# mLSTM gates by lanes of a direction, head and block of 128 tokens in place of rows

## The chip, the cores and the metric

One Trainium2 chip, one core. The number that counts is the device time of one execution of the kernel in microseconds (us). TensorE (PE) does matmuls and transposes, VectorE (DVE), ScalarE (ACT) and GpSimd (POOL) do elementwise work, SyncE (SP) and ACT issue the DMAs of this kernel. Each engine works through its own list of instructions in order and waits on semaphores for the others.

## The reference

Two layers of a backbone over 256 context tokens and 1024 latent tokens (1280 in all, ten tiles of 128), width 1024. Each layer normalizes, projects into the inputs of four head groups and a gate path, runs the groups, and projects back. The change touches the second group, the bidirectional mLSTM with four heads of 64:

```python
def _mlstm_step(state, xs):
    ...
    b = jnp.cumsum(lf, axis=-1)
    d = jnp.where(tril, b[..., :, None] - b[..., None, :] + li[..., None, :], -jnp.inf)
    m_inter = b + m[..., None]
    m_t = jnp.maximum(m_inter, jnp.max(d, axis=-1))
    w = jnp.exp(d - m_t[..., None])
    g_inter = jnp.exp(m_inter - m_t)
    ...
    h = num / jnp.maximum(jnp.abs(nq), jnp.exp(-m_t))[..., None]
    ...
    w_end = jnp.exp(g - m_new[..., None])
    decay = jnp.exp(b_end + m - m_new)
...
def mlstm_mixer(pl, pc, conv_w, conv_b, gate_b, outn_g, with_ctx):
    ...
        qk = jax.nn.silu(short_conv(jnp.concatenate([q, k], axis=-1), conv_w, conv_b))
    ...
        fwd = base + (pre[0], jax.nn.log_sigmoid(pre[1]))
        bwd = base + (pre[2], jax.nn.log_sigmoid(pre[3]))
```

Per token, direction and head there are an input gate `li` and a forget gate `lf`. What the recurrence needs of them is a running sum `b` of the log forget gates, a running maximum `m_t`, and four exponentials made from these.

## The kernel before

Each layer is a row of stages (modulation, norm, mLSTM, GLA, differential attention, window attention, gates, output) with a barrier of all engines behind each, and the engine programs in a stage are written out by hand. The mLSTM stage (`stage_mlstm`) has three blocks, each again ended by all engines: the projection block (the one changed), the recurrence over ten tiles in two directions, and `turn_out`.

The projection block runs `SplitProduct`, a product of the activations `hT` with weights in float32 split in a high and a low part. It has four groups of eight steps, written (g, k) here and in the code. In each step ACT makes the high part of the activations (`high`, tile `b_proj_xh`), DVE makes the high and low parts of the weights and the low part of the activations (`low`, tiles `b_proj_wh`, `b_proj_wl`, `b_proj_xl`), and PE multiplies (`multiply`). There are two buffers, so ACT and DVE may prepare step i when PE has finished step i-2. Groups 0 and 1 make the values `v` and the gates for five tiles of tokens each, with `WV` weight columns (15 matmuls a step). Groups 2 and 3 make the keys and the queries, transposed, for all 1280 tokens (18 matmuls a step, 12 with 512 columns and 6 with 256). The sums of a group are kept by ACT (`keep`) in the next group's step 1, behind that step's `high`; PE's first matmul of a group waits for the first of them, since the sums rotate through six PSUM banks.

Between the steps stand other pieces. In group 2 PE turns the gates into rows (`turn_gates`), 36 rows with 8 in use (direction and head) and 1280 tokens each, ACT adds the bias (`keep_gates`) and starts log sigmoid, DVE sums over each tile (`gate_sums`, behind `low` of (2, 6)) and runs the maxima and the joins of the tile ends (`gate_rows`, behind `low` of (3, 0)). Then DVE convolves the keys (`convolve`, behind (3, 2) and (3, 4)) and finishes their silu (`silu_k`, behind (3, 5) and (3, 7)). Behind the last step stand: the convolutions and silu of the queries on DVE; on PE 40 turns of the gate rows back to tokens, a small product for `decay`, and 20 turns of the keys; on ACT two sigmoids, the exponentials of the gates (16 pieces) and ten copies of turned keys (`ktm`).

The order is thus fixed by hand through the place of each piece between the steps, for example:

```python
                    if (g, k) == (2, 6):
                        gate_sums()
                    if (g, k) == (3, 0):
                        gate_rows()
```

Of the kernel before, what the change touches and what calls it, by code (L numbers as in the profile page):

```python
# [42 lines left out]
ROWS = 36  # L43
BLOCKS = [(0, 512), (512, 512), (1024, 256)]
# [8 lines left out]
SLAB_W = [512] * 4 + [328, 512, 288, 256, 512, 256, 512, 256, 512, 512] + [512] * 2 + [512] * 2  # L53
# [431 lines left out]
def stage_mlstm(nc, env):  # L485
    ps, signal, yT, ring = (env[n] for n in ("ps", "signal", "yT", "ring"))
    outer = ExitStack()
    with outer:
        v1 = outer.enter_context(env["sbuf"]("b_v", [P, NT, HEADS, DH + 1], F32))
        qkT = outer.enter_context(env["sbuf"]("b_qkT", [P, 4, T], F32))  # L490

        after = lambda s_, n: ring[:, s_ % RING, KT * SLAB_W[s_]:KT * SLAB_W[s_] + n]
        cols = after(S_CQK, NT * 4 * ROWS).rearrange("p (t q r) -> p t q r", t=NT, q=4)
        row_d = after(S_CV, T)[0:ROWS, :]
        row_a, row_c, row_e, row_b = (yT[0:ROWS, i, :] for i in range(4))
# [1954 lines left out]
```

## Time and profile before

| | us |
|---|---|
| median of 3 runs | 2687.75 |
| fastest, slowest | 2673.01, 2691.18 |
| the profiled execution | 2683.7 |
| its span in the trace | 2681.9 |
| projection block, layer 0 | 64.5 to 221.2 |
| projection block, layer 1 | 1435.3 to 1588.0 |

Times in rows are from the start of the profiled execution's span. Over the whole span PE is busy for 80% and DVE for 70%, but these are averages over stages with different limits; the projection blocks have to be read by themselves. A granted clock of TensorE is given as a share of full speed, 2.4 GHz.

### The profile page before, as it was taken

Reading aid. Unit: us, or ns where it says so; the run is one execution under the profiler, and the core shown is the slowest. Engines: PE = TensorE matmul, PEld = TensorE weight load, DVE = VectorE, ACT = ScalarE, POOL = GpSimd, SP = SyncE. Lnnn points to the kernel's source line nnn. Section 1 sums busy time; section 2 is a strip of 40 time slices with the busy share of each in tenths; the row PEclk is TensorE's granted clock in tenths of the full one; section 3 lists DMA queues with packets and bytes.
Section 4 is the critical chain, followed back from the end, with each engine's and each line's share of the span. In section 5 each row is a group of like instructions: output and inputs, shape, how many; then the busy total and the mean of one; then the engine's idle time right before and its main releaser. Section 6 shows DMA issues by size and latency. Waiting matters only on the chain. (4 is left out here: it accounts for less than half of the span.)

```text
span 2681.9 us, 38569 instructions
## 1 busy us (share of the span) xinstructions
PE 2151.8 (80%) x14712; PEld 1804.3 (67%) x14712; DVE 1867.3 (70%) x3533; ACT 1129.8 (42%) x2196; POOL 411.4 (15%) x410
## 2 busy tenths in 40 slices
PE   4968798786888785899978778879767977858988
PEld 2857676666677664787857567767655866647877
DVE  2585667778878567755745766669698786667757
ACT  4433351333667534633224443432435666346321
POOL 0002204322000011022110004025031000110222
PEclk7978896898898797999988889969788989979999
DMA  8100010000000100001433000100000001000021
GB/s 322 74 16 1 17 48 2 2 1 1 1 1 1 48 32 1 29 36 39 153 138 120 16 16 2 48 16 2 1 0 1 1 1 48 16 17 27 37 104 54
DMA packets 18182, 99.80 MB, mean 37 GB/s; under 512 B 2128, under 2 KB 2256, under 8 KB 12752
## 3 DMA queue, kind: packets, MB, share of 16 engines
q1 hardware_dynamic: 12816, 87.89, 8.6%
q10 hardware_dynamic: 5184, 9.44, 0.9%
q8 instruction: 119, 1.95, 0.3%
q14 instruction: 63, 0.52, 0.1%
HBM read 87.88 MB, written 9.44 MB: 36 GB/s over the span
## 5 line engine op out<-in xcount | busy, mean ns | idle before, releaser
L1807 DVE TENSOR_REDUCE a_st<-ps 128x1 f32<-128x1280 f32 (+1 forms) x144 | 196.9, 1370 | 23.2 <-PE ps L1719 22.7
L1778 ACT ACTIVATE ring<-ps,a_st 128x1280 f32<-128x1280 f32 (+1 forms) x144 | 177.3, 1232 | 74.6 <-DVE a_st L1807 74.4
L454 PE MATMUL ps<-a_proj_wh,a_proj_xh 128*128 128x512 f32 (+1 forms) x320 | 119.2, 373 | 62.5 <-DVE a_proj_xl L435 61.6
L2090 PE MATMUL ps<-g_x_hi,g_w_hi 128*128 128x512 f32 (+1 forms) x400 | 148.4, 371 | 10.0 <-DVE g_x_lo L2151 9.5
L2091 PE MATMUL ps<-g_x_lo,g_w_hi 128*128 128x512 f32 (+1 forms) x400 | 147.7, 369 | 0.0
L2092 PE MATMUL ps<-g_x_hi,g_w_lo 128*128 128x512 f32 (+1 forms) x400 | 147.6, 369 | 0.0
L1719 PE MATMUL ps<-a_k,a_q 128*128 128x512 f32 (+1 forms) x400 | 123.8, 419 | 26.1 <-ACT ring L1778 21.6
L2151 DVE TENSOR_TENSOR g_x_lo<-hT,g_x_hi 128x512 fp32r<-128x512 f32 (+1 forms) x120 | 84.5, 709 | 85.3 <-ACT g_x_hi L2114 83.8
L2114 ACT ACTIVATE g_x_hi<-hT 128x512 fp32r<-128x512 f32 (+1 forms) x120 | 70.3, 589 | 158.3 <-PE ps L2092 151.2
L1734 PE MATMUL ps<-cst,ring 128*128 128x128 f32 x656 | 107.8, 299 | 27.0 <-ACT a_aT L1787 15.1
L418 ACT ACTIVATE b_proj_xh<-hT 128x640 fp32r<-128x640 f32 (+1 forms) x64 | 63.8, 1003 | 147.4 <-PE ps L454 145.0
L2225 PE MATMUL ps<-o_w_hi,o_y_hi 128*128 128x512 f32 x288 | 114.1, 396 | 13.5 <-DVE o_y_lo L2256 7.2
L2164 POOL TENSOR_TENSOR yT<-yT,g_gate 128x512 f32<-128x512 f32 (+1 forms) x50 | 61.3, 1232 | 382.5 <-DVE g_gate L2129 236.7
L454 PEld LDWEIGHTS ps<-a_proj_wh,a_proj_xh 128*128 128x128 f32 x320 | 68.7, 215 | 75.3 <-issue 48.9
L454 PE MATMUL ps<-a_proj_wl,a_proj_xh 128*128 128x512 f32 (+1 forms) x320 | 116.2, 363 | 0.0
L454 PE MATMUL ps<-a_proj_wh,a_proj_xl 128*128 128x512 f32 (+1 forms) x320 | 115.8, 362 | 0.0
L2226 PE MATMUL ps<-o_w_lo,o_y_hi 128*128 128x512 f32 x288 | 113.5, 394 | 0.0
L2227 PE MATMUL ps<-o_w_hi,o_y_lo 128*128 128x512 f32 x288 | 113.3, 393 | 0.0
L1734 PEld LDWEIGHTS ps<-cst,ring 128*128 128x128 f32 x656 | 81.4, 153 | 46.5 <-ACT a_aT L1787 22.9
L454 PE MATMUL ps<-b_proj_xh,b_proj_wh 128*128 128x512 f32 (+1 forms) x192 | 76.9, 401 | 44.4 <-DVE b_proj_xl L435 38.0
L418 ACT ACTIVATE a_proj_xh<-hT 128x640 fp32r<-128x640 f32 x64 | 46.6, 741 | 147.9 <-PE ps L454 145.6
L2282 ACT ACTIVATE o_y_hi<-yT 128x640 fp32r<-128x640 f32 (+1 forms) x64 | 43.5, 686 | 152.5 <-PE ps L2227 144.6
(363 smaller groups left out, 6397.9 us busy)
## 6 DMA issues: line engine op xcount, KB each, us to landing
ring<-in_w SPq DMA_DIRECT2D x22, 2048.0 KB, 7.5
yT<-in_w SPq DMA_DIRECT2D x4, 2048.0 KB, 9.8
latents<-hT ACTq DMA_DIRECT2D x32, 256.0 KB, 2.0
ring<-in_w SPq DMA_DIRECT2D x6, 1024.0 KB, 5.0
hT<-in_tok SPq DMA_DIRECT2D x10, 512.0 KB, 15.5
hT<-in_tok SPq DMA_DIRECT2D x20, 256.0 KB, 5.9
hT<-latents SPq DMA_DIRECT2D x16, 256.0 KB, 6.5
cst<-in_cst SPq DMA_DIRECT2D x1, 2688.0 KB, 14.6
```

What stands on the lines that cost most here:

```text
L418: act.activation(self.x_hi[:, i % self.BUFS, 0:m], self.env["hT"][:, k, t0:t0 + m], ACT.Copy).then_inc(self.hi.sem, 1)
L454: last = pe.matmul(out, left, right, start=k == 0 and j == 0, stop=k == KT - 1 and j == 2)
L1719: last = pe.matmul(ps[:, 3 * c + b, 0:w], q4[:, 2 * h + c, t * P:(t + 1) * P], k4[:, 2 * h + c, k0:k0 + w], start=True, stop=True)
L1734: last = pe.transpose(ps[:, 6 + n % 2, (k - a) * P:(k - a + 1) * P], p(u, 0, T)[:, k * P:(k + 1) * P], C(env, "ident"))
L1778: act.activation(p(u, c, n), ps[:, 3 * c:3 * c + 3, :].rearrange("p b n -> p (b n)")[:, 0:n], ACT.Exp, bias=st[:, 0:1], accum_out=st[:, 1: ...
L1807: dve.tensor_reduce(stat[:, u % SLOTS, c, 0:1], ps[:, 3 * c:3 * c + 3, :].rearrange("p b n -> p (b n)")[:, 0:n], AX.X, ALU.max, negate=Tru ...
L2090: pe.matmul(out, w_hi[:, k, cols], x_hi[:, at, 0:b[1]], start=k == 0, stop=False)
L2091: pe.matmul(out, w_hi[:, k, cols], x_lo[:, at, 0:b[1]], start=False, stop=False)
L2092: last = pe.matmul(out, w_lo[:, k, cols], x_hi[:, at, 0:b[1]], start=False, stop=k == KT - 1)
L2225: pe.matmul(ps[:, n % 8, :], y_hi[:, at, tile], w_hi[:, at, :], start=k == 0, stop=False)
L2226: pe.matmul(ps[:, n % 8, :], y_hi[:, at, tile], w_lo[:, at, :], start=False, stop=False)
L2227: last = pe.matmul(ps[:, n % 8, :], y_lo[:, at, tile], w_hi[:, at, :], start=False, stop=k == KT - 1)
```

## The change

The gates no longer stand as 8 rows of 1280 tokens but as lanes: one partition for each direction, head and tile of 128 tokens, 104 partitions wide with 80 in use (40 of a direction from partition 0, 40 from partition 64), each 128 long. The projection makes 16 gate columns without gaps, so `WV` is 272 in place of 328. ACT puts the gates of a tile into four columns a direction of `gt`, and two transposes turn all of them. The sums and the maxima within a tile are then four scans of 40 lanes by 128. The ends of the tiles are joined on 36 rows by 10: `ends_by_row` moves each lane's end to its row and tile through a product with a 0/1 matrix (`lane_row`), `tile_peaks` runs the maxima over ten tiles, and `back_to_lanes` brings the results back through `row_lane`. The exponentials are taken on lanes (`exps`, in ACT's place (3, 0)), where ACT also issues 20 DMAs, each of 4 partitions by 128 elements, that bring one quantity (`g_cm`) back to rows for the recurrence. Four transposes turn the lanes to tokens (`turn_lanes`, PE's place (3, 1)), and two ACT instructions keep them (`keep_lanes`). The keys are turned two tiles at a time into a bank of their own and kept by five ACT instructions between the sigmoids of the queries. POOL clears two more pieces of `yT`.

```diff
-SLAB_W = [512] * 4 + [328, 512, 288, 256, 512, 256, 512, 256, 512, 512] + [512] * 2 + [512] * 2
+SLAB_W = [512] * 4 + [272, 512, 288, 256, 512, 256, 512, 256, 512, 512] + [512] * 2 + [512] * 2
...
-        after = lambda s_, n: ring[:, s_ % RING, KT * SLAB_W[s_]:KT * SLAB_W[s_] + n]
...
+        cols = ring[:, S_CV % RING, KT * SLAB_W[S_CV]:KT * SLAB_W[S_CV] + 4 * LANES].rearrange("p (q r) -> p q r", q=4)
+        lane_at = lambda i: yT[0:LANES, 0, i * P:(i + 1) * P]
+        g_a, g_b, g_t, g_c, g_e, g_m, g_cm, g_inter, g_floor, g_end = (lane_at(i) for i in range(10))
+        row_b = yT[0:ROWS, 3, :]
         ends = outer.enter_context(env["sbuf"]("b_ends", [ROWS, 4, NT], F32))
         decay = outer.enter_context(env["sbuf"]("b_decay", [P, 4, NT], F32))
-        conv_in = yT[:, 4:8, :]
+        conv_in = [yT[:, c, :] for c in (1, 2, 6, 7)]
         ktm = yT[:, 4:6, :].rearrange("p a t -> p (a t)").rearrange("p (t c) -> p t c", t=NT)
         hB = yT[:, 0:2, :].rearrange("p a t -> p (a t)").rearrange("p (t h d) -> p t h d", t=NT, h=HEADS)
-        gt = yT[:, 7, 0:NT * 2 * ROWS].rearrange("p (t r) -> p t r", t=NT)
+        gt = yT[:, 7, 0:2 * P].rearrange("p (q r) -> p q r", q=2)
+        gt_of = lambda t: gt.rearrange("p q (w r) -> p q w r", w=2)[:, :, :, 4 * t:4 * t + 4]
...
-        WV = GW + 2 * ROWS
+        WV = GW + 4 * HEADS
...
-                def turn_gates(n):
...
+                def turn_gates():
+                    pe.wait_ge(proj.read.sem, NT)
+                    pe.wait_ge(mod_kept.sem, 2)
+                    for q in range(2):
+                        last = pe.transpose(ps[0:LANES, 6, q * P:(q + 1) * P], gt[:, q, 0:LANES], C(env, "ident"))
                     last.then_inc(gates_turned.sem, 1)
+                def ends_by_row():
+                    pe.wait_ge(ends_cut.sem, 4)
+                    pe.matmul(ps[0:ROWS, 7, 0:2 * NT], C(env, "lane_row", LANES), cut_at[0:LANES, :, :].rearrange("p a t -> p (a t)"),
+                              start=True, stop=True).then_inc(ends_mm.sem, 1)
+                def back_to_lanes():
+                    pe.wait_ge(peaks_ready.sem, 1)
+                    pe.matmul(ps[0:LANES, 7, P:P + 2 * NT], C(env, "row_lane", ROWS),
+                              ends[:, 0:3:2, :], start=True, stop=True, skip_group_check=True).then_inc(back_mm.sem, 1)
+                def turn_lanes():
+                    pe.wait_ge(lane_exps.sem, 4)
+                    pe.wait_ge(lanes_ready.sem, 1)
+                    for q, x in enumerate((g_a, g_inter, g_floor, g_end)):
+                        last = pe.transpose(ps[:, 6, q * LANES:(q + 1) * LANES], x, C(env, "ident")[0:LANES, 0:LANES])
+                    last.then_inc(lanes_turned.sem, 1)
...
+                def keep_gates():
+                    act.wait_ge(v_ones.sem, 4)
+                    act.wait_ge(gates_turned.sem, 1)
+                    act.activation(g_a, ps[0:LANES, 6, 0:P], ACT.Identity, bias=W(env, "gate_li", LANES)).then_inc(act_l.sem, 1)
+                    act_l.n += 1
+                    act_l.link(act, act.activation(g_b, ps[0:LANES, 6, P:2 * P], ACT.Identity, bias=W(env, "gate_lf", LANES)))
+                    act_l.link(act, act.activation(g_t, g_b, ACT.Abs))
+                    act_l.link(act, act.activation(g_t, g_t, ACT.Exp, scale=-1.0))
+                    act_l.mark(act.activation(g_t, g_t, ACT.Ln, bias=1.0))
+                def exps():
+                    act.wait_ge(lanes_ready.sem, 1)
+                    act.activation(g_inter, g_cm, ACT.Exp, bias=lane_ends[0:LANES, 1:2]).then_inc(lane_exps.sem, 1)
+                    act.activation(g_floor, g_m, ACT.Exp, scale=-1.0).then_inc(lane_exps.sem, 1)
+                    act.activation(g_end, g_a, ACT.Exp, bias=lane_ends[0:LANES, 0:1]).then_inc(lane_exps.sem, 1)
+                    act.activation(ends[:, 3, :], ends[:, 3, :], ACT.Exp).then_inc(lane_exps.sem, 1)
+                    for way in range(2):
+                        for t in range(NT):
+                            act.dma_start(row_b[32 * way:32 * way + HEADS, t * P:(t + 1) * P],
+                                          g_cm[64 * way + HEADS * t:64 * way + HEADS * (t + 1), :]).then_inc(row_moved.sem, 16)
+                def keep_lanes():
+                    act.wait_ge(lanes_turned.sem, 1)
+                    act.activation(cols[:, :, :], ps[:, 6, 0:4 * LANES].rearrange("p (q r) -> p q r", q=4), ACT.Copy).then_inc(lanes_kept.sem, 1)
+                    act.wait_ge(lanes_turned.sem, 2)
+                    act.activation(decay[:, :, :], ps[:, 7, 0:4 * NT].rearrange("p (a b) -> p a b", a=4), ACT.Copy).then_inc(lanes_kept.sem, 1)
+                def keep_k(n):
+                    act.wait_ge(turned.sem, n + 1)
+                    act.activation(ktm[:, 2 * n:2 * n + 2, :].rearrange("p t c -> p (t c)"), ps[:, 6 + n % 2, :], ACT.Copy).then_inc(turned_kept.sem, 1)
...
-                    if g == 2 and k in (2, 3, 4):
...
+                    if (g, k) == (2, 2):
+                        keep_gates()
+                    if (g, k) == (3, 0):
+                        exps()
+                    if (g, k) == (3, 2):
+                        keep_lanes()
                     if g == 3 and k in (4, 6):
                         sigmoid(2 if k == 4 else 3)
                 for n in range(proj.first[-2], proj.first[-1]):
                     keep(n)
-                for c in range(2):
...
+                keep_k(0)
+                keep_k(1)
+                sigmoid(0)
+                keep_k(2)
+                sigmoid(1)
+                keep_k(3)
+                keep_k(4)
+                act.wait_ge(turned_kept.sem, NT // 2)
+                act.wait_ge(row_moved.sem, 2 * NT * 16)
...
-                    dve.wait_ge(act_l.sem, 3)
                     dve.wait_ge(env["const_loaded"].sem, 16)
-                    dv.link(dve, dve.scalar_tensor_tensor(out=row_b, in0=row_b, scalar=0.0, in1=row_c,
...
+                    dve.wait_ge(act_l.sem, 5)
+                    dv.link(dve, dve.scalar_tensor_tensor(out=g_b, in0=g_b, scalar=0.0, in1=g_t, op0=ALU.min, op1=ALU.subtract))
+                    ones, tiles = C(env, "ones"), C(env, "lane_tile")
+                    for i, (r, at) in enumerate(WAYS):
+                        x = (lambda y: y[r, :]) if i == 0 else (lambda y: y[r, ::-1])
+                        dv.mark(dve.tensor_tensor_scan(x(g_c), ones[r, :], x(g_b), 0.0, ALU.mult, ALU.add))
+                        dv.link(dve, dve.tensor_tensor_scan(x(g_e), x(g_b), x(g_a), NEG, ALU.add, ALU.max))
+                        for j, y in enumerate((g_c, g_e)):
+                            dve.tensor_scalar(cut_at[r, j, :], tiles[r, :], y[r, at:at + 1], None, ALU.mult).then_inc(ends_cut.sem, 1)
+                def tile_peaks():
+                    dve.wait_ge(ends_mm.sem, 1)
+                    dv.mark(dve.memset(ends[:, 1:4, :], 0.0))
+                    dv.link(dve, dve.tensor_copy(ends[:, 0, :], ps[0:ROWS, 7, 0:NT]))
+                    c, e, m = ends[:, 0, :], ps[0:ROWS, 7, NT:2 * NT], ends[:, 1, :]
+                    b = slice(32, ROWS)
+                    dv.mark(dve.tensor_tensor_scan(m[0:HEADS, :], c[0:HEADS, :], e[0:HEADS, :], 0.0, ALU.add, ALU.max))
+                    dv.link(dve, dve.tensor_tensor_scan(m[b, 0:NC][:, ::-1], c[b, 0:NC][:, ::-1], e[b, 0:NC][:, ::-1], 0.0, ALU.add, ALU.max))
+                    dv.link(dve, dve.tensor_tensor_scan(m[b, NC:NT][:, ::-1], c[b, NC:NT][:, ::-1], e[b, NC:NT][:, ::-1],
+                                                        m[b, 0:1], ALU.add, ALU.max))
...
                     dv.link(dve, dve.tensor_tensor(ends[:, 0, :], ends[:, 0, :], ends[:, 1, :], ALU.subtract))
                     dv.link(dve, dve.tensor_tensor(ends[:, 3, :], ends[:, 0, :], ends[:, 2, :], ALU.add))
-                    wide = lambda i: ends[:, i, :].unsqueeze(2).broadcast_to([ROWS, NT, P])
...
+                    dve.sem_inc(peaks_ready.sem, 1)
+                def lanes():
+                    dve.wait_ge(back_mm.sem, 1)
+                    r = slice(0, LANES)
+                    dv.mark(dve.tensor_tensor(g_a, g_a, g_c, ALU.subtract))
+                    dv.link(dve, dve.tensor_tensor(back[r, :, :], ps[r, 7, P:P + 2 * NT].rearrange("p (a t) -> p a t", a=2),
+                                                   C(env, "lane_tile", LANES).unsqueeze(1).broadcast_to([LANES, 2, NT]), ALU.mult))
+                    dv.link(dve, dve.tensor_reduce(lane_ends[r, :], back[r, :, :], AX.X, ALU.add))
+                    dv.link(dve, dve.scalar_tensor_tensor(out=g_m, in0=g_c, scalar=lane_ends[r, 1:2], in1=g_e, op0=ALU.add, op1=ALU.max))
+                    dv.link(dve, dve.tensor_tensor(g_cm, g_c, g_m, ALU.subtract))
+                    dve.sem_inc(lanes_ready.sem, 1)
 
...
+                dv.link(dve, dve.memset(cut_at[:, :, :], 0.0))
                 for n in range(2):
                     dve.memset(ps[:, 6 + n, :], 0.0).then_inc(mod_cleared.sem, 1)
                 for i, (g, k) in enumerate(proj.steps):
                     proj.low(dve, i)
-                    if (g, k) == (2, 6):
+                    if (g, k) == (2, 3):
                         gate_sums()
-                    if (g, k) == (3, 0):
-                        gate_rows()
+                    if (g, k) == (2, 5):
+                        tile_peaks()
+                    if (g, k) == (2, 7):
+                        lanes()
...
-                return cols[:, j, q, 32 * way:32 * way + HEADS]
+                return cols[:, q, 64 * way + HEADS * j:64 * way + HEADS * (j + 1)]
...
+                lane, row = 64 * way + HEADS * t + h, 32 * way + h
+                put("lane_row")[lane, row] = 1.0
+                put("row_lane")[row, lane] = 1.0
+                put("lane_tile")[lane, t] = 1.0
...
-        slabs += [np.concatenate([take(*B_V), li, lf], 1), take(*B_QK),
+        slabs += [np.concatenate([take(*B_V)] + [gates[:, i] for i in (0, 2, 1, 3)], 1), take(*B_QK),
```

The first place is DVE behind `low` of (2, 6) and (3, 0), before (`yT`, `ring` hold the gate rows, `b_ends` the tile ends):

```order
L674 SCALAR_TENSOR_TENSOR yT<-yT 36x1280
...
L681 SCALAR_TENSOR_TENSOR yT<-cst,yT 4x128
L683 SCALAR_TENSOR_TENSOR yT<-cst,yT 4x128
...
L687 SCALAR_TENSOR_TENSOR ring<-yT 4x1280
L689 SCALAR_TENSOR_TENSOR ring<-yT 4x256
L691 SCALAR_TENSOR_TENSOR ring<-yT,ring 4x1024
...
L706 TENSOR_TENSOR yT<-yT 36x1280
L707 TENSOR_TENSOR yT<-yT,ring 36x1280
L708 TENSOR_TENSOR yT<-yT,b_ends 36x1280
L709 TENSOR_TENSOR yT<-yT,b_ends 36x1280
```

The same engine in the changed kernel, behind `low` of (2, 3) and of (2, 7) (`b_cut` and `b_back` are the operands of the 0/1 products):

```order
L706 SCALAR_TENSOR_TENSOR yT<-yT 104x128
L710 SCALAR_TENSOR_TENSOR yT<-cst,yT 40x128
L711 SCALAR_TENSOR_TENSOR yT<-yT 40x128
L713 TENSOR_SCALAR b_cut<-cst,yT 40x10 x2
...
L736 TENSOR_TENSOR yT<-yT 104x128
L737 TENSOR_TENSOR b_back<-ps,cst 104x20
L739 TENSOR_REDUCE b_lane_ends<-b_back 104x2
L740 SCALAR_TENSOR_TENSOR yT<-yT,b_lane_ends 104x128
L741 TENSOR_TENSOR yT<-yT 104x128
```

The long rows became short ones, in three pieces in place of two (behind (2, 5) stand eleven more of at most 36 by 30), all of them behind steps of group 2.

The second place is ACT between the `high` of (3, 0) and of (3, 1) in the changed kernel; before, nothing stood there:

```order
L633 ACT_TABLE_LOAD
L633 ACTIVATE yT<-yT,b_lane_ends 104x128
L634 ACTIVATE yT<-yT 104x128
L635 ACTIVATE yT<-yT,b_lane_ends 104x128
L636 ACTIVATE b_ends<-b_ends 36x10
L639 DMA yT<-yT 4x128 x20
L420 ACTIVATE b_proj_xh<-hT 128x1280
```

So the exponentials and 20 DMA issues now stand ahead of that `high`. The third place is ACT behind the last kept sums, before:

```order
L613 ACTIVATE yT<-b_qkT 128x1280 x2
L638 ACT_TABLE_LOAD
L638 ACTIVATE b_ends<-b_ends 36x10
L644 ACTIVATE ring<-ps 128x3x36 x12
L644 ACTIVATE ring<-ps 128x36 x4
L647 ACTIVATE b_decay<-ps 128x40
L651 ACTIVATE yT<-ps 128x256 x10
```

and in the changed kernel:

```order
L650 ACTIVATE yT<-ps 128x512 x2
L655 ACTIVATE yT<-b_qkT 128x1280
L650 ACTIVATE yT<-ps 128x512
L655 ACTIVATE yT<-b_qkT 128x1280
L650 ACTIVATE yT<-ps 128x512 x2
```

Nothing of the gates is left there, and of the ten copies of keys five wider ones, three of them ahead of the second sigmoid.

## Rows read from the trace of the kernel before

**Rows 1.** Windows, both layers: length, busy PE, PEld, DVE, ACT, POOL (instructions), PE clock, DMA.

```profile
64.50:106.80 42.30, 38.66 (x245) 36.44 (x249) 25.95 (x50) 13.78 (x27) 0.17 (x1) 0.92 0.31 117
...
158.60:203.40 44.80, 35.26 (x145) 29.04 (x145) 36.82 (x51) 17.96 (x22) 0.00 (x0) 0.81 0.07 24
203.40:221.20 17.80, 8.62 (x68) 8.17 (x68) 10.19 (x11) 9.76 (x31) 0.05 (x1) 0.62 0.00 0
...
1435.30:1476.60 41.30, 37.77 (x245) 35.57 (x249) 25.95 (x50) 13.69 (x27) 0.07 (x1) 0.96 0.31 120
...
1528.00:1569.70 41.70, 32.01 (x144) 26.36 (x144) 37.14 (x51) 18.05 (x22) 0.00 (x0) 0.92 0.08 26
```

**Rows 2.** DVE's timeline in group 0, and in the GLA stage's like group.

```profile
76.72 0.33 DVE L381 CAST b_proj_wh<-ring 128x328 fp32r<-128x328 f32 x1 [0.63 <-PE ps L454]
...
87.94 0.33 DVE L381 CAST b_proj_wh<-ring 128x328 fp32r<-128x328 f32 x1 [0.64 <-PE ps L454]
...
328.18 0.83 DVE L435 TENSOR_TENSOR c_proj_xl<-hT,c_proj_xh 128x640 fp32r<-128x640 f32 x1
...
340.24 0.83 DVE L435 TENSOR_TENSOR c_proj_xl<-hT,c_proj_xh 128x640 fp32r<-128x640 f32 x1
```

**Rows 3.** DVE's timeline, gate pieces of layer 0, start and length in us.

```profile
138.19 1.48 DVE L674 SCALAR_TENSOR_TENSOR yT<-yT 36x1280 f32<-36x1280 f32 x1
...
141.20 0.41 DVE L681 TENSOR_TENSOR_SCAN yT<-cst,yT 4x128 f32<-4x128 f32 x1
...
154.22 2.80 DVE L687 TENSOR_TENSOR_SCAN ring<-yT 4x1280 f32<-4x1280 f32 x1
...
160.15 0.16 DVE L695 COPY b_ends<-yT 4x10 f32<-4x10 f32 x1
...
166.04 1.48 DVE L709 TENSOR_TENSOR yT<-yT,b_ends 36x1280 f32<-36x1280 f32 x1
...
171.81 0.94 DVE L661 TENSOR_SCALAR b_qkT<-yT,par 128x1280 f32<-128x1280 f32 x1
```

**Rows 4.** PE's timeline: turns, (2, 7), (3, 0), (3, 6) and (3, 7).

```profile
119.11 1.04 PE L548 MATMUL ps<-cst,yT 128*36 128x128 f32 x8
...
152.39 0.76 PE L454 MATMUL ps<-b_proj_xh,b_proj_wh 128*128 128x512 f32 x1 [10.23 <-DVE b_proj_xl L435]
...
160.54 0.47 PE L454 MATMUL ps<-b_proj_xh,b_proj_wh 128*128 128x512 f32 x1 [1.94 <-ACT yT L598]
...
195.65 0.40 PE L454 MATMUL ps<-b_proj_xh,b_proj_wh 128*128 128x512 f32 x1
...
199.15 0.39 PE L454 MATMUL ps<-b_proj_xh,b_proj_wh 128*128 128x512 f32 x1
```

**Rows 5.** Window of step (2, 7), columns as in rows 1.

```profile
152.40:158.50 6.10, 6.10 (x18) 4.89 (x18) 6.00 (x6) 0.00 (x0) 0.00 (x0) 0.55 0.00 0
```

**Rows 6.** ACT's timeline: a `high`, and pieces at the end of the block.

```profile
158.64 1.27 ACT L418 ACTIVATE b_proj_xh<-hT 128x1280 fp32r<-128x1280 f32 x1 [15.17 <-PE ps L454]
...
212.42 1.28 ACT L638 ACT_TABLE_LOAD   x1
...
216.98 3.73 ACT L651 ACTIVATE yT<-ps 128x256 f32<-128x256 f32 x10 [0.84 <-PE ps L583]
```

**Rows 7.** DVE's timeline from the queries' convolution to the next block.

```profile
201.64 0.95 DVE L661 TENSOR_SCALAR b_qkT<-yT,par 128x1280 f32<-128x1280 f32 x1 [1.60 <-ACT yT L598]
...
211.19 2.89 DVE L734 TENSOR_TENSOR b_qkT<-b_qkT,yT 128x1280 f32<-128x1280 f32 x2
221.18 1.05 DVE L876 CAST b_row_parts<-yT 64x1280 fp32r<-64x1280 f32 x1 [7.09 <-PEq L516]
```

**Rows 8.** DMA issues by line: duration ns min/median/max, first and last start.

```profile
L2276 ACTq DMA_DIRECT2D latents<-hT x32: 338/338/374, 1309.6 to 2678.5; - x32
...
DMA to landing us min/median/max: 2.0/2.0/3.9
...
L2203 SPq DMA_DIRECT2D hT<-in_tok x20: 327/432/678, 1271.3 to 1281.1; - x20
```

More of the change, by code:

```diff
@@ L43 @@
 ROWS = 36
+LANES = 104
 BLOCKS = [(0, 512), (512, 512), (1024, 256)]
@@ new lines, in turn_lanes @@
+                def turn_lanes():
[4 more added lines that the diff above has]
+                    last.then_inc(lanes_turned.sem, 1)
+                    sel = C(env, "sel_pair", ROWS).rearrange("p (a b) -> p a b", a=4)
+                    for i in range(4):
+                        last = pe.matmul(ps[:, 7, i * NT:(i + 1) * NT], sel[:, i, :], ends[:, 3, :], start=True, stop=True)
+                    last.then_inc(lanes_turned.sem, 1)
@@ L558, in _ @@
                         modulate(pe, env, mod_w[:, k - 5, :, :], k + 1).then_inc(mod_mm.sem, 1)
-                    if g == 2 and k in (1, 2, 3):
-                        turn_gates(k - 1)
-                pe.wait_ge(proj.read.sem, proj.first[-1])
-                pe.wait_ge(rows_ready.sem, 1)
-                for t in range(NT):
-                    for q, r in enumerate((row_a, row_c, row_d, row_e)):
-                        at = (t % 3) * 4 * ROWS + q * ROWS
-                        last = pe.transpose(ps[:, 4 + t // 3, at:at + ROWS], r[:, t * P:(t + 1) * P],
-                                            C(env, "ident")[0:ROWS, 0:ROWS])
-                last.then_inc(turned.sem, 1)
-                pe.wait_ge(dec_ready.sem, 1)
-                sel = C(env, "sel_pair", ROWS).rearrange("p (a b) -> p a b", a=4)
-                for i in range(4):
-                    last = pe.matmul(ps[:, 0, i * NT:(i + 1) * NT], sel[:, i, :], ends[:, 3, :], start=True, stop=True)
-                last.then_inc(turned.sem, 1)
-                pe.wait_ge(silu_ready.sem, 4)
-                for t in range(NT):
-                    if t == 0:
-                        pe.wait_ge(turned_kept.sem, 17)
-                    if t >= 4:
-                        pe.wait_ge(turned_kept.sem, 17 + t - 3)
-                    for c in range(2):
-                        last = pe.transpose(ps[:, t % 4, c * P:(c + 1) * P], qkT[:, 2 + c, t * P:(t + 1) * P], C(env, "ident"))
+                    if (g, k) == (2, 1):
+                        turn_gates()
+                    if (g, k) == (2, 4):
+                        ends_by_row()
+                    if (g, k) == (2, 6):
+                        back_to_lanes()
+                    if (g, k) == (3, 1):
+                        turn_lanes()
+                pe.wait_ge(lanes_kept.sem, 2)
+                pe.wait_ge(silu_ready.sem, 2)
+                for n in range(NT // 2):
+                    if n >= 2:
+                        pe.wait_ge(turned_kept.sem, n - 1)
+                    for i in range(4):
+                        t, c = 2 * n + i // 2, i % 2
+                        last = pe.transpose(ps[:, 6 + n % 2, i * P:(i + 1) * P], qkT[:, 2 + c, t * P:(t + 1) * P], C(env, "ident"))
                     last.then_inc(turned.sem, 1)
@@ L2333, in constants @@
     put("ones")[:] = 1.0
+    for way in range(2):
+        for t in range(NT):
+            for h in range(HEADS):
+                lane, row = 64 * way + HEADS * t + h, 32 * way + h
+                put("lane_row")[lane, row] = 1.0
+                put("row_lane")[row, lane] = 1.0
+                put("lane_tile")[lane, t] = 1.0
     put("diag")[:] = (np.arange(P)[:, None] // 32) == (np.arange(GW)[None, :] // DH)
```

124 lines of the change are left out of this document (31 added, 93 removed).

## The prediction

> **What bounds the kernel now.** The change touches one block of one stage in each layer, and every block is ended by all engines together, so what that block loses or gains goes into the total one to one. I read it from the windows first [rows 1]: in the stretch of group 3 PE is busy 35.26 of 44.80 us and DVE 36.82, at a granted clock of 0.81, so neither is full and they take turns; in the last 17.80 us PE has 8.62 and DVE 10.19, a chain. In groups 0 and 1 PE is busy 38.66 of 42.30. The timelines say who sets the pace. In group 0 DVE's weight cast comes every 2.24 us (11.22 us over five steps) and waits for PE each time [rows 2]: PE is the bound. In group 2 PE stands 10.23 us before step (2, 7) for DVE's `low` [rows 4], because `gate_sums` runs on DVE from 138.19 [rows 3]; the low clock follows, and that step takes 6.10 us at clock 0.55 [rows 5], where a step at full clock takes 3.50 (195.65 to 199.15 [rows 4]). `gate_rows` then holds DVE from 154.22 to 167.5 [rows 3]. At the end DVE finishes the queries at 214.08 (211.19 + 2.89), but the next block starts at 221.18 [rows 7]: the last 7.1 us are ACT's exponentials and key copies, begun by a table load at 212.42 and ended by copies from 216.98 [rows 6].
>
> **Groups 0 and 1: narrower product.** `WV` goes from 328 to 272. The nearest row is the GLA stage, 288 columns: six steps from 328.18 to 340.24, 2.01 a step [rows 2]. Forty columns cost 0.23, so 272 gives 2.01 - 0.09 = 1.92, and a step gains 0.33. DVE's and ACT's work for a step (about 1.6) stays under that. Over 15 steps: **4.9 us a layer**. Bounds: 3.5 (0.23 a step, the price of 288 columns) to 5.7 (2.24 us over 328 columns, 0.0068 a column).
>
> **Group 2: the gate pieces, in layer 0's time, groups 0 and 1 left as they were.** Prices: a DVE step is 2.15 (two steps between 167.5 and 171.81 [rows 3]), `high` 1.27 [rows 6], a scan of 128 0.41 plus 0.03, a tiny DVE instruction 0.16 [rows 3], an ACT instruction of 128 columns 0.26 (from 1.27 for 1280 and 0.37 for 256 columns [rows 6]), a table load 1.28. The path:
> - (2, 1) ends on PE at 119.11, where the turns start. Eight turns took 0.8 of PE; two take 0.3. ACT then does five instructions and one table load, 119.75 to 122.5, and `high` of (2, 3) ends at 123.8; `low` at 125.25; PE runs (2, 3) 125.3 to 128.8.
> - `gate_sums` (0.3 + 4 scans + 4 tiny) 2.7 us to 127.95; `low` of (2, 4) to 130.1; PE 130.1 to 133.6, then the first 0/1 product to 133.85. `low` of (2, 5) is done at 132.2, so DVE idles 1.8 for that product.
> - `tile_peaks`, eleven tiny instructions, 1.75: to 135.75. `low` of (2, 6) to 137.9; PE (2, 5) to 137.4, (2, 6) to 141.4, the second product to 141.6. DVE waits again, 1.8.
> - `lanes`, five instructions, 1.25: to 143.05; PE (2, 7) from 141.6 to 145.1, ahead of DVE.
>
> So the long idle and its low clock are gone from (2, 7): 145.1 against 158.4. What is late next is ACT. `exps` waits for `lanes` (143.05), loads a table, does four instructions: 145.5. Then it issues 20 DMAs before `high` of (3, 1). An issue on ACT took 0.338 of its own [rows 8]; SP's run of 20 took 10.2 from first start to end, 0.51 each. These rows are all DMAs of 128 partitions; one of 4 partitions is in no row. I take 0.39 (0.338 and a gap of 0.05), since 0.33 is the floor whatever the bytes: 7.8 us, to 153.3. `high` starts then, and PE starts (3, 0) 1.90 behind it (158.64 to 160.54 [rows 4, 6]): 155.2 in place of 160.5, **gain 5.3**. Bounds for an issue: 0.05 (nothing but a gap), giving 148.4, and 0.51, giving 157.6.
>
> The Trainium skill, DMA: Bandwidth & Descriptors, section Anatomy of one DMA, gives for GpSimd's path about 50 ns of sequencer dispatch, with descriptor generation "small, variable". By that the 20 issues would cost 1.0 us and the gain of group 2 would be 12.1; the trace's issues from ACT and SP do not agree, at 0.33 and more.
>
> **Group 3.** From the start of (3, 0), T0. PE stood 10 us, so as at (2, 7) [rows 5] (3, 0) takes 6.0. DVE's `low` of (3, 2) waits for it and for `high`: done at T0 + 8.75. Convolution 4.75 (9.55 for two [rows 7]) to 13.5, `low` to 15.6, `low` of (3, 4) to 17.75, convolution to 22.5, `low` 24.65, silu 26.1, `low` 28.25; PE is then the bound, (3, 6) to 31.75 and (3, 7) behind it; the queries' convolution starts 2.5 later (199.15 to 201.64 [rows 4, 7]), at T0 + 34.25. Before it was T0 + 41.1: **gain 6.8** in layer 0. `turn_lanes` (about 1.0 on PE) and `keep_lanes` (0.8 on ACT) stand behind (3, 1) and (3, 2), where PE waits 1.6 for the convolution anyway: they cost nothing; without that cover 1.8.
>
> **The end.** The keys' turns and three of five copies lie under the 9.5 us of convolution; no exponentials remain. DVE's last product ends 12.45 behind the convolution's start as now (214.08 - 201.64 [rows 7]); barrier 0.4. 12.85 in place of 19.54: **gain 6.7**. The recurrence's first exponential needs a table load in the next block, where ACT waits for PE's warm-up. That warm-up follows a longer rest of PE: cost 0.5, bounds 0 and 2. The Trainium skill, ScalarE: Activation LUTs, section What ACT_TABLE_LOAD costs, adds a drain of about 1.38 us to each load; here the load took 1.28 and nothing more stood behind it [rows 6], so I leave it out. With it the load in `exps` would cost 1.4 more a layer, the sum 2.8 less.
>
> **The sum.** Layer 0: 4.9 + 5.3 + 6.8 + 6.7 - 0.5 = 23.2, so its block goes from 156.7 to 133.5. Layer 1's block was 152.7: it lost less to the clock, 1.4 in groups 0 and 1 (0.96 against 0.92 [rows 1]) which the changed kernel will save again, and 3.1 in group 3 (a stretch of 41.70 against 44.80, at 0.92 against 0.81 [rows 1]). Its new length is 133.5 - 1.4 = 132.1, gain 20.6. Together **43.8**: the profiled execution from 2683.7 to 2639.9. That execution lies 4 us below the median, so against the median 2687.75 the forecast is **2644**.
>
> **Rivals.**
> - **Issues are cheap.** Four partitions need fewer descriptors and fewer rings than any row. At 0.05 the issues are over at 146.5, T0 is 148.4, 6.8 earlier, and PE's rest is 3 us, so perhaps (3, 0) runs at full clock (2.5 more). Gain 43.8 + 13.6 to 18.6, time **2625 to 2630**. For it: nothing measured at that size. Against: no issue in [rows 8] took under 0.327.
> - **The short pieces are slow to hand over.** Three crossings DVE-PE-DVE and some 25 tiny instructions stand in line in group 2; 0.2 more for each is 5 us a layer, time **2654**. Against: tiny ones follow each other at 0.1 to 0.2.
> - **The clock stays low in group 3.** If it stays at 1.2 GHz in place of 2.4 after the rest in front of (3, 0), eight steps of 6.1 make it PE-bound: 48.8 + 2.5 against 34.25, reduced by what overlaps to 14 a layer; time **2672**. For it: 0.81 in layer 0. Against: 0.92 in layer 1 with the same rests [rows 1].
> - **Slower: the issues queue.** If each issue must wait until the one before has landed, 2.0 us [rows 8], 20 of them take 40 in place of 7.8 on ACT, T0 moves by 32 a layer, time **2708**. It decides from 1.5 us an issue on (0.39 + 22/20). Against: ACT's stores land in 2.0 but hold it 0.34.
> - **Nothing gained but the width**: if a wait I have not seen, such as the row transfers at the block's end, covers the rest: 2678.
>
> **How the numbers follow.** Forecast (2636 to 2650) 0.50; cheap issues 0.25; slow handovers 0.13; low clock 0.06; queued issues 0.03; only the width 0.03. The range from 2622 to 2660 leaves out the last three. A change of 1% (27 us, about what a measurement of this kernel can tell from none) is at 2661: faster 0.88, same 0.08, slower 0.04.
>
> **What the profile after will show.** Step period 1.92 in group 0; PE's start of (2, 7) without a wait of 10 us; 20 issues on ACT between `high` of (3, 0) and of (3, 1), with PE idle behind them for 10 us (rival one: 3); 12.9 from the queries' convolution to the next block. Wrong it would be made by the price of an issue above all: each 0.1 is 4 us of the total. Next is the clock in group 3, 2.5 us for each slow step on the path.

## The result and the profile after

The changed kernel takes **2638.94 us** (median of 4, 2634.85 to 2641.88), the kernel before 2684.22 on the same chip (median of 4): ratio 0.9833, 95% interval 0.9806 to 0.986, 45.3 us less. The forecast was 2644. One execution that is read below, the profiled one of the eight longer issues, ran at a granted clock of 0.54 throughout and took 3546 us; it counts in no median. The profiled execution of the changed kernel took 2636.4. The head of its page, then the new issues on ACT's queue, by line:

```profile
span 2634.6 us, 38349 instructions
PE 2109.6 (80%) x14612; PEld 1765.6 (67%) x14612; DVE 1827.8 (69%) x3505; ACT 1117.2 (42%) x2156; POOL 413.4 (16%) x414
L639 ACTq DMA_DIRECT2D yT<-yT x40: 584/585/1180, 139.9 to 1500.9; - x40
```

The shares are averages over all stages and say little here. The last line says most: each new issue held ACT for 0.585 us (584/585/1180 are minimum, median and maximum in ns). Layer 0's block by windows, in place of [rows 1]: groups 0 and 1, group 2, the rest in front of (3, 0), group 3, the end (busy time and count of PE, PEld, DVE, ACT, POOL, then the granted clock, the DMA share and GB/s):

```profile
66.20:104.40 38.20, 36.29 (x261) 32.36 (x262) 25.95 (x50) 14.26 (x27) 0.36 (x1) 0.91 0.34 135
104.40:141.20 36.80, 32.93 (x163) 27.10 (x162) 23.13 (x50) 17.06 (x30) 1.98 (x2) 0.95 0.00 1
141.20:154.69 13.49, 0.02 (x1) 0.03 (x1) 1.38 (x4) 1.90 (x3) 0.00 (x0) 0.63 0.01 3
154.69:188.40 33.71, 30.77 (x151) 25.80 (x152) 25.21 (x31) 15.32 (x19) 0.00 (x0) 0.95 0.09 32
188.40:201.30 12.90, 3.84 (x27) 2.92 (x25) 11.86 (x12) 6.48 (x10) 0.00 (x0) 0.79 0.00 0
```

One hole is left, the third row: 13.5 us in which no engine does much. The timeline of ACT names its owner:

```profile
137.29 1.27 ACT L420 ACTIVATE b_proj_xh<-hT 128x1280 fp32r<-128x1280 f32 x1 [2.96 <-PE ps L456]
138.59 1.28 ACT L633 ACT_TABLE_LOAD   x1
139.88 0.40 ACT L633 ACTIVATE yT<-yT,b_lane_ends 104x128 f32<-104x128 f32 x1
...
140.69 0.19 ACT L636 ACTIVATE b_ends<-b_ends 36x10 f32<-36x10 f32 x1
141.10 11.64 ACTq L639 DMA_DIRECT2D yT<-yT  x19
152.79 1.27 ACT L420 ACTIVATE b_proj_xh<-hT 128x1280 fp32r<-128x1280 f32 x1 [11.91 <-issue]
```

On PE's timeline, the turns of the gates in layer 0 and the first matmul of (3, 0) in layer 1:

```profile
114.14 0.38 PE L554 MATMUL ps<-cst,yT 128*104 128x128 f32 x2
...
1503.46 0.77 PE L456 MATMUL ps<-b_proj_xh,b_proj_wh 128*128 128x512 f32 x1 [12.91 <-ACT yT L618]
```

PE rested 12.91 us in front of (3, 0) in layer 1. DVE's timeline gives the step pitch of group 0, one short piece of each kind in group 2, the queries' convolution and the next block's first row in each layer (answering to [rows 2, 3, 7]):

```profile
77.83 0.30 DVE L383 CAST b_proj_wh<-ring 128x272 fp32r<-128x272 f32 x1 [0.41 <-PE ps L456]
...
85.62 0.30 DVE L383 CAST b_proj_wh<-ring 128x272 fp32r<-128x272 f32 x1 [0.39 <-PE ps L456]
...
120.48 0.42 DVE L710 TENSOR_TENSOR_SCAN yT<-cst,yT 40x128 f32<-40x128 f32 x1
...
129.41 0.08 DVE L717 MEMSET b_ends<- 36x30 f32 x1 [0.90 <-PE ps L559]
...
137.58 0.29 DVE L736 TENSOR_TENSOR yT<-yT 104x128 f32<-104x128 f32 x1 [1.72 <-PE ps L564]
...
188.41 0.95 DVE L693 TENSOR_SCALAR b_qkT<-yT,par 128x1280 f32<-128x1280 f32 x1 [1.59 <-ACT yT L618]
...
201.37 1.04 DVE L911 CAST b_row_parts<-yT 64x1280 fp32r<-64x1280 f32 x1 [0.53 <-PEq L521]
...
1549.91 1.04 DVE L911 CAST b_row_parts<-yT 64x1280 fp32r<-64x1280 f32 x1 [0.53 <-PEq L521]
```

The block took 201.37 - 64.5 = 136.9 us (before 156.7) and in layer 1, begun at 1415.3, 134.6 (before 152.7): 19.8 and 18.1 us less, 37.9 together, where I had forecast 43.8. The spans differ by 47.3. So the block gave less than forecast, and something outside it gave 9.4.

### The profile page after: what moved, and what is told of

Same layout as the page of the kernel before. It is cut to its first block and busy times, and to the rows that moved or that the text cites. A ratio compares the mean times of both kernels' runs of the same rounds, so it can differ in the third digit from the quotient of the medians.

```text
span 2634.6 us, 38349 instructions
## 1 busy us (share of the span) xinstructions
PE 2109.6 (80%) x14612; PEld 1765.6 (67%) x14612; DVE 1827.8 (69%) x3505; ACT 1117.2 (42%) x2156; POOL 413.4 (16%) x414
## 5 line engine op out<-in xcount | busy, mean ns | idle before, releaser
L1754 PE MATMUL ps<-a_k,a_q 128*128 128x512 f32 (+1 forms) x400 | 123.8, 419 | 25.8 <-ACT ring L1813 21.3
L1241 ACT ACTIVATE yT<-ps 128x1024 f32<-128x1024 f32 x40 | 41.0, 1024 | 153.5 <-PE ps L1259 153.5
```

Of the source, the lines that this page charges most:

```text
L1754: last = pe.matmul(ps[:, 3 * c + b, 0:w], q4[:, 2 * h + c, t * P:(t + 1) * P], k4[:, 2 * h + c, k0:k0 + w], start=True, stop=True)
```

## Experiments

Unless said otherwise each differs from the changed kernel by the edit shown, and "more" or "less" is against its median, 2638.94. The kernel before had medians of 2679.64 and 2679.13 beside the experiments, 5 us below the 2684.22 beside the changed kernel, so a difference of totals alone is good to about 5 us. What the two projection blocks took in the profiled execution of each kernel is a second measure. It agrees with the totals to 3 us, except for the kernel before:

| kernel | layer 0 | layer 1 | both, against the changed kernel | total, against it |
|---|---|---|---|---|
| before | 156.7 | 152.8 | +37.9 | +45.3 (more on it at the end of this section) |
| changed | 136.9 | 134.6 | | |
| issues on SP | 123.7 | 125.1 | -22.8 | -24.3 |
| 8 issues on SP | 125.0 | 123.8 | -22.8 | -23.6 |
| 20 more issues | 147.5 | 148.0 | +24.0 | +25.3 |
| width given back | 142.4 | 141.2 | +12.0 | +12.3 |
| rest kept warm | 136.6 | 134.5 | -0.5 | +2.1 |
| turns at the end | 140.7 | 138.7 | +7.9 | +7.7 |

**The issues on SP,** between its loads of the values' and the keys' weights, and taken out of `exps`.

```diff
+                sp.wait_ge(lanes_ready.sem, 1)
+                for way in range(2):
+                    for t in range(NT):
+                        sp.dma_start(row_b[32 * way:32 * way + HEADS, t * P:(t + 1) * P],
+                                      g_cm[64 * way + HEADS * t:64 * way + HEADS * (t + 1), :]).then_inc(row_moved.sem, 16)
...
-                            act.dma_start(row_b[32 * way:32 * way + HEADS, t * P:(t + 1) * P],
```

> The changed kernel with its 20 row transfers issued by SP in place of ACT, behind SP's wait for the lanes. Theory (the issues hold ACT, and ACT's high of (3, 1) holds PE): the rest of PE in front of (3, 0) falls from 13.5 us to about 2, since (2, 7) ended at 141.2 and a high and the first kept sum take 1.9; (3, 0) starts at about 143.2 in place of 154.7, and runs at full clock. Gain 11.5 to 14 us a layer, 23 to 28 together, time 2611 to 2616 where the changed kernel has 2639. Rival (the transfers or the exponentials, not the issues, hold the chain): the start of (3, 0) stays within 2 us of 154.7 and the time within 5 of 2639.

Measured 2614.65 (2612.82 to 2617.13), ratio 0.9756 (0.9742 to 0.9771) to the kernel before, 24.3 less than the changed one. SP's issues, PE's first matmul of (3, 0), and the next block:

```profile
L537 SPq DMA_DIRECT2D yT<-yT x40: 577/577/712, 137.2 to 1485.9; - x40
...
141.34 0.47 PE L456 MATMUL ps<-b_proj_xh,b_proj_wh 128*128 128x512 f32 x1 [1.94 <-ACT yT L624]
...
187.88 1.05 DVE L913 CAST b_row_parts<-yT 64x1280 fp32r<-64x1280 f32 x1 [0.54 <-PEq L521]
```

An issue costs SP the same 0.577, and nobody waits for it. PE's rest is 1.94 us in place of 13.5, and the next block of layer 0 comes 13.5 earlier. The 20 issues in ACT's path are what the changed kernel left lying: 12 us a layer (13.2 and 9.6 by the blocks). One part of the expectation failed: (3, 0) did not run at full clock, see the warm rest below.

**Fewer, longer issues:** 8 of 10 partitions into one, still on ACT.

```diff
-                        for t in range(NT):
-                            act.dma_start(row_b[32 * way:32 * way + HEADS, t * P:(t + 1) * P],
-                                          g_cm[64 * way + HEADS * t:64 * way + HEADS * (t + 1), :])
+                        for h in range(HEADS):
+                            act.dma_start(row_b[32 * way + h:32 * way + h + 1, :].rearrange("p (t i) -> p t i", t=NT),
+                                          g_cm[64 * way + h:64 * way + HEADS * NT:HEADS, :])
```

> The changed kernel with 8 transfers on ACT in place of 20, the same data: one for each direction and head, from 10 partitions (one for each tile) to one partition. Theory (a fixed price for each issue, 0.585 in the changed kernel): 8 of them take about 4.9 us in place of 12.3, (3, 0) starts about 7.3 earlier, gain 15 together, 2624. Rival (the price goes with rows or descriptors, 80 in both): an issue takes about 1.4, nothing is gained, 2639.

```profile
L639 ACTq DMA_DIRECT2D yT<-yT x16: 725/731/1324, 176.4 to 2000.6; - x16
```

Measured 2626.03 (2624.28 to 2628.41), ratio 0.9797 (0.9781 to 0.9813), 12.9 less, where the fixed price of 0.585 promised 15. Of its profile only the issues count. An issue of this shape costs 0.73, neither 0.585 nor the 1.4 of the rival; 8 x 0.73 is 5.8 in place of 12: half of what SP gives. Both steps together, these 8 on SP:

> The changed kernel with 8 transfers, one for each direction and head, issued by SP. If the issues on ACT were all that held (3, 0), it is as fast as 20 issues from SP, 2611 to 2616; if the transfers' end or the load of the next slab behind them on SP matters, it is some us faster than that.

```profile
L537 SPq DMA_DIRECT2D yT<-yT x16: 718/719/850, 138.7 to 1485.0; - x16
```

Measured 2615.3 (2613.02 to 2616.14), the same as 20 on SP, and the two blocks together are the same too. Between 8 and 20 on SP the number of issues has no price.

**What an issue costs by kind:** 20 more issues on ACT behind the 20, four of each kind, to unused places: 4, 16, 128 and 1 partitions from SBUF, then 4 partitions from DRAM. The first and the last of the five loops:

```diff
+                    for n in range(4):
+                        act.dma_start(spare(slice(0, 4), n), C(env, "ident", 4)).then_inc(kinds.sem, 16)
...
+                    for n in range(4):
+                        act.dma_start(spare(slice(0, 4), 16 + n), env["dram"]["cst"][0:4, 0:P]).then_inc(kinds.sem, 16)
```

> The changed kernel with 20 more issues on ACT behind the first 20, four each of five kinds, of constants into a spare place: 4 partitions inside SBUF, 16 partitions inside SBUF, 128 partitions inside SBUF, 1 partition inside SBUF, 4 partitions from DRAM; each row 512 B. It measures the price of an issue by kind. If the number of partitions sets it: 4 partitions 0.585 in both places, 128 partitions 0.34. If SBUF to SBUF sets it: all four kinds inside SBUF 0.585 and the one from DRAM about 0.33. The whole gets about 12 us slower a layer, 2663.

Measured 2664.26 in one run, 25.3 more. The rows are in the order of the kinds:

```profile
L643 ACTq DMA_DIRECT2D yT<-cst x8: 584/585/585, 151.1 to 1516.3; - x8
...
L645 ACTq DMA_DIRECT2D yT<-cst x8: 556/608/611, 153.6 to 1518.8; - x8
...
L647 ACTq DMA_DIRECT2D yT<-cst x8: 612/622/629, 156.1 to 1521.3; - x8
...
L649 ACTq DMA_DIRECT2D yT<-cst x8: 611/613/622, 158.7 to 1523.9; - x8
...
L651 ACTq DMA_DIRECT2D yT<-in_cst x8: 287/317/698, 161.2 to 1525.8; - x8
```

Partitions hardly count. What counts is where the ends lie, by this run: medians of 0.585 to 0.622 with both in SBUF, 0.317 with the source in DRAM. The first of the four from DRAM took 0.70 in layer 0, so the four held ACT for 1.76 us there and 1.58 in layer 1, still less than the 2.5 of any other kind. All of [rows 8] had an end in DRAM; that is why their 0.338 did not carry over. It is one run, though, and the kind from DRAM stood last in both layers.

**The width given back:** 328 columns again, 56 of them zeros.

```diff
-SLAB_W = [512] * 4 + [272, 512, 288, 256, 512, 256, 512, 256, 512, 512] + [512] * 2 + [512] * 2
+SLAB_W = [512] * 4 + [328, 512, 288, 256, 512, 256, 512, 256, 512, 512] + [512] * 2 + [512] * 2
-        WV = GW + 4 * HEADS
+        WV = GW + 18 * HEADS
```

> The changed kernel with the product of groups 0 and 1 as wide as before, 328 columns, 56 of them zero weights that nobody reads. Theory (4.9 us a layer come from the width): 10 us slower, 2649, a step of group 0 at 2.24 in place of 1.95. Rival (PE's rest in front of (2, 0) or DVE takes the gain up): within 3 us of 2639.

```profile
76.40 0.33 DVE L383 CAST b_proj_wh<-ring 128x328 fp32r<-128x328 f32 x1 [0.63 <-PE ps L456]
...
78.64 0.33 DVE L383 CAST b_proj_wh<-ring 128x328 fp32r<-128x328 f32 x1 [0.64 <-PE ps L456]
...
206.42 1.04 DVE L911 CAST b_row_parts<-yT 64x1280 fp32r<-64x1280 f32 x1 [0.53 <-PEq L521]
```

Measured 2651.2 (2648.85 to 2653.62), 12.3 more: the pitch is 2.24 again and layer 0's block ends 5.05 later. The term of the width holds.

**The rest kept warm:** 12 products that nobody reads, behind (2, 7), to hold TensorE's clock up while ACT issues.

```diff
+                    if (g, k) == (2, 7):
+                        pe.wait_ge(act_l.sem, 5)
+                        for n in range(12):
+                            pe.matmul(ps[:, 6, :], C(env, "ident"), C(env, "sel_row")[:, 0:512], start=True, stop=True)
```

> The changed kernel with 12 idle matmuls of 512 columns in float32 on PE behind step (2, 7), into a bank that is free, so that PE does not rest through the 13.5 us in which ACT issues. Theory (the granted clock falls while PE rests, and (3, 0) takes 6.0 in place of 3.5 for it): (3, 0) starts at the same time and takes 3.5; gain 2.5 a layer, 5 together, 2634. Rival (the first slow step is covered by DVE): no difference.

Windows of the 12 products' stretch, of what rest is left, and of (3, 0):

```profile
139.40:149.90 10.50, 10.42 (x25) 4.30 (x24) 0.87 (x3) 0.00 (x0) 0.00 (x0) 1.00 0.01 3
149.90:152.99 3.09, 0.00 (x1) 0.04 (x1) 0.60 (x1) 1.90 (x3) 0.00 (x0) 1.00 0.01 2
152.99:158.30 5.31, 5.31 (x19) 4.50 (x20) 0.89 (x1) 1.86 (x5) 0.00 (x0) 0.68 0.00 0
```

Measured 2641.05 (2637.87 to 2641.92): nothing gained. After 10.5 busy us at clock 1.00 and 3.1 of rest, (3, 0) still took 5.1 us to the start of (3, 1) (the window holds one matmul more), against 5.3 and 5.0 in the changed kernel's two layers. So the long rest is not needed to make (3, 0) slow. The kernel before showed it already: there (3, 0) followed a rest of 1.94 us, with the clock at 1.00 up to its start, and took 5.1. But the short rest doesn't settle it either. With issues on SP (3, 0) stood behind the same 1.94 us in all four blocks; it took 5.1 in three of them, and in layer 1 with 8 issues it ran at full clock. (3, 0) before, in layer 0, then in that block:

```profile
160.54:165.66 5.12, 5.12 (x18) 4.22 (x18) 4.88 (x11) 1.87 (x5) 0.00 (x0) 0.67 0.01 3
...
1483.63:1487.20 3.57, 3.57 (x19) 3.05 (x20) 0.90 (x1) 1.87 (x5) 0.00 (x0) 1.00 0.03 6
```

What decides between 3.6 and 5.1 stays open.

**The turns of the lanes at the end** (`turn_lanes`, `keep_lanes` and all key copies behind the last step).

```diff
-                    if (g, k) == (3, 1):
-                        turn_lanes()
+                turn_lanes()
-                    if (g, k) == (3, 2):
-                        keep_lanes()
-                keep_k(0)
-                keep_k(1)
                 sigmoid(0)
-                keep_k(2)
                 sigmoid(1)
-                keep_k(3)
-                keep_k(4)
+                keep_lanes()
+                for n in range(5):
+                    keep_k(n)
```

> The changed kernel with the gates' way to tokens (turn_lanes, keep_lanes) and all five key copies moved behind the sigmoids at the end of the block, where they stood before the change, still as few and as wide as in the changed kernel. Theory (the end of 6.6 us was ACT's list behind the second sigmoid): ACT ends at 199.2 + 0.5 + 0.2 + 2.7 = 202.6 plus a wait, DVE at 200.8, so 2 us a layer slower, 4 together, 2643; the other 4.6 us of each end come from fewer instructions and no exponentials. Rival (the order is what counts): 13 us slower, 2652.

PE's 20 key turns, a copy that waits for its pair of turns, and the next block:

```profile
199.65 4.62 PE L600 MATMUL ps<-cst,b_qkT 128*128 128x128 f32 x20 [8.80 <-ACT b_decay L645]
...
200.81 0.60 ACT L649 ACTIVATE yT<-ps 128x512 f32<-128x512 f32 x1 [1.21 <-PE ps L600]
...
205.38 1.04 DVE L906 CAST b_row_parts<-yT 64x1280 fp32r<-64x1280 f32 x1 [4.60 <-PEq L521]
```

Measured 2646.64 (2644.55 to 2648.44), 7.7 more, 4.0 a layer by the block's end: between the 4 of the theory and the 13 of the rival, nearer the theory. The key turns wait 8.80 us for `keep_lanes`, and each copy then for its turns. DVE waits 4.60 for the end of the block: the end had no slack beyond its 0.53. The edit moved the key copies as well, so the 4 is the price of both covers together; it does not price `turn_lanes` and `keep_lanes` alone, on which I had put 1.8.

**The same two kernels once more**, for the 9 us outside the blocks:

> The kernel before once more, for its stages. Between the traces of before and after the span differs by 47.3 us, the two projection blocks only by 38.1; some 8 us of the rest lie in layer 1's differential attention, whose code is the same: 378.1 us from its first activation cast to that of the next projection before, 369.9 after. Theory (chance of an execution): this stage takes 370 to 378 us here, and may well take 370. Rival (what ran ahead of it, the changed block, sets it): 378 again, within 1.

> The changed kernel once more. Chance: the same stage takes anything from 370 to 378 us, and where it takes 378 the run is longer by as much. Rival: 370 again, within 1. In both, the projection blocks end 19.8 and 18.1 us earlier than in the kernel before, within 1.

Both ran once, at 2679.33 and 2641.86. The blocks by part, for both executions of each kernel: from the block's first activation cast to PE's start of (3, 0), group 3 from there to the queries' convolution, the end, the whole.

| kernel, execution, layer | to (3, 0) | group 3 | end | block |
|---|---|---|---|---|
| before, first, 0 | 96.0 | 41.1 | 19.5 | 156.7 |
| before, first, 1 | 94.7 | 38.1 | 20.0 | 152.8 |
| before, again, 0 | 94.5 | 38.1 | 20.0 | 152.6 |
| before, again, 1 | 96.4 | 39.6 | 20.0 | 156.0 |
| changed, first, 0 | 90.2 | 33.7 | 13.0 | 136.9 |
| changed, first, 1 | 88.2 | 33.5 | 13.0 | 134.6 |
| changed, again, 0 | 88.7 | 34.8 | 13.0 | 136.4 |
| changed, again, 1 | 88.2 | 33.5 | 13.0 | 134.7 |

Here I missed: the blocks give 16.2 and 21.3 us in the second pair, not 19.8 and 18.1 within 1. The kernel before's long block lies in layer 0 once and in layer 1 the other time. Only the sum of both layers is steady, 37.9 and 37.5 us, and a term of one layer is good to some 4 us.

Layer 1's differential attention (first activation cast to the next projection's) took 1896.3 to 2274.4 = 378.1 us in the kernel before, the same as in its first profile: the rival's 378 within 1. In the changed kernel it took 371.2 after 369.9, just outside 1. In the kernels of the other experiments it took 369.9 to 371.2, but 376.5 with 8 issues on SP. Other stages whose code is the same move as well: the GLA stage of layer 0 took 218.4 and 213.2 us in the kernel before, and that of layer 1 took 208.9 with 8 issues on SP against 216 to 217 in both kernels here. Windows of the attention follow, of the kernel before and then of the changed kernel, both in their first profiles. In each pair the second row is the stage's second part as a whole, the first row 24 us of it, from 120 us behind its start:

```profile
2136.20:2160.20 24.00, 18.74 (x93) 16.70 (x94) 10.60 (x26) 6.79 (x14) 3.95 (x6) 0.62 0.00 0
2016.20:2278.90 262.70, 204.50 (x1373) 179.25 (x1373) 204.03 (x314) 164.40 (x300) 13.16 (x20) 0.88 0.03 13
```

```profile
2099.90:2123.90 24.00, 16.28 (x110) 13.76 (x109) 17.97 (x42) 9.36 (x20) 6.58 (x10) 0.86 0.00 1
1979.90:2233.40 253.50, 196.06 (x1373) 170.88 (x1373) 202.95 (x310) 164.52 (x300) 13.16 (x20) 0.92 0.04 13
```

The same 1373 matmuls take PE 204.5 us at clock 0.88 or 196.1 at 0.92; DVE's and ACT's work is equal. The drop to 0.62 in the first row, against 0.86, is what one form has and the other not. That both profiles of the kernel before have it speaks against mere chance of an execution, but two are few; that one kernel with the changed code has the long form too (8 issues on SP: 205.1 us at 0.88) speaks against the changed kernel as such. What decides stays open.

## Why the prediction was right, and where it was not

The time came out 5 us from the forecast, partly by luck. The two blocks gave 37.9 us where the sum had 43.8, because one term was 4.4 us too good in layer 0; outside them came 9.4 us that stand in no term, 8.2 of them in layer 1's attention. And 3.5 of the 5 us are not the change's: the kernel before's median went from 2687.75 to 2684.22 with its fourth run, and the gain itself was 45.3 for 43.8. Term by term, layer 0, first profiles:

| term | forecast | measured |
|---|---|---|
| groups 0 and 1 | 4.9 | 5.0 |
| group 2, to the start of (3, 0) | 5.3 | 0.9 |
| group 3 | 6.8 | 7.4 |
| the end | 6.7 | 6.6 |
| warm-up of the next block | -0.5 | -0.1 |

The last row is from the next block's start to the GLA stage. By the same measure layer 1 lost 1.1 us, and the second pair of profiles 1.8 and 2.0, so the loss there was rather 1 than 0.5; how much of it is the warm-up isn't shown. Group 3 gave 7.4 in this block and 4.6, 3.3 and 6.2 in the other three.

- **Width: right.** Pitch (85.62 - 77.83) / 4 = 1.95 for 1.92; (2, 1) ended 4.97 us earlier, and giving the width back cost 12.3 for two layers, 2 more than the term.
- **The pieces of group 2: right.** `gate_sums` took 2.7 us, `tile_peaks` 1.8, and the last exponential ended at 140.88 where the working gives 145.5 - 4.9 = 140.6. The rival of slow handovers is out: DVE waited 0.90 and 1.72 for the two 0/1 products, I had said 1.8 each.
- **"I take 0.39 (0.338 and a gap of 0.05)": the step that failed.** From the last exponential's end (140.88) to the next `high` (152.79) it was 11.9 us, not 7.8; nineteen issues in a row took 11.64, 0.61 each, outside my bounds of 0.05 to 0.51. PE started (3, 0) at 154.69, where the working gives 155.2 - 4.9 = 150.3. A fixed price whatever the bytes had the right form, but 0.33 is that of another kind of transfer: [rows 8] has only DMAs with an end in DRAM, and I took the partitions for what was new in mine, when it was the place of its ends. The rival of cheap issues went the wrong way. So does the rule weighed there: the Trainium skill, DMA: Bandwidth & Descriptors, section Anatomy of one DMA, gives about 50 ns of dispatch for GpSimd's path. No DMA here goes by that path, so the figure itself isn't tested; but taken over to ACT and SP it doesn't hold. The least median of a kind was 0.317 on ACT, and 0.328 on SP for its loads of weights.
- **Group 3: right, for a part with the wrong cause.** (3, 0) was slow as forecast (5.3 for 6.0; 5.0 to 6.3 over the four blocks), but the step at fault in the working is "PE stood 10 us, so as at (2, 7)": the kernel before's own (3, 0) took 5.1 behind 1.94 us of rest, and 12 products in the rest changed nothing. From there PE kept up, and the clock of 0.95 over the stretch put the rival of a low clock out. The smaller loss to the clock that I gave layer 1 of the kernel before was not the layer's: in the second profile layer 0 had the short block.
- **The end: right.** 12.96 for 12.85, and no exponentials in it. Without their cover the lanes' turns and the key copies together cost 4; the 1.8 for the turns alone was not tested.
- **The table load: right.** In `exps` it stood from 138.59, 0.03 us behind the `high` ahead of it, for 1.28 us, and the first exponential began at 139.88; so the drain of about 1.38 us that the Trainium skill adds behind a load (ScalarE: Activation LUTs, What ACT_TABLE_LOAD costs) is not in the trace. [rows 6] does not show what followed the load in the kernel before; there an exponential began at 213.72, 0.02 us behind it.

## What to carry to other kernels

A DMA is also an instruction of the engine that issues it. Before small transfers go on a queue, look for a row of the same kind, both ends in the same kinds of memory, and count issues times that, on an engine whose next step others wait for. If no such row exists, put them on an engine with nothing to do: moving 20 issues a layer from ACT to SP gave 24 us on top of the change's 45. And when a sum comes out right, compare it by stage, and in a second profile of each kernel: here two misses of opposite sign made the total, and the parts of one layer moved by 4 us from one execution to the next with no change of code.

## What the runs showed of the hardware

- An issue holds ACT or SP for a median of 0.577 to 0.622 us when both ends are in SBUF, from 1 to 128 partitions, 0.73 (ACT) and 0.72 (SP) when ten partitions go into one, and 0.317 on ACT when the source is in DRAM.
- (3, 0) takes 3.5 us at full clock (2.4 GHz). Behind a rest of 1.94 us, with the clock at 1.00 up to its start, it took 5.1 us in both layers of the kernel before, at 0.67, and in three of four blocks with the issues on SP; in the fourth it took 3.57 at 1.00. In the slow ones the clock fell to the lower level, 1.2 GHz, at the step's start or within it, and rose again before its end.
- Behind a rest of about 13 us, through which the mean clock was 0.59 to 0.70, the same step took 5.0 to 6.4 us.
- The same 1373 matmuls of a stage took 204.5 or 196.1 us of PE, by the clock granted to them. Of one kernel, unchanged, a block took 156.7 us and then 152.6.
